# Two-layer diffusion trunk: per-token sums of squares of the differential attention by ScalarE, values turned back on TensorE, swapped rope rows by DMA, maps turned three blocks behind their scores

## What is computed

```python
q, k, v = split(h @ w_in, 3)
q = q * d ** -0.5                      # d = 64
q, k = rope(q), rope(k)                # latent tokens only; rotates pairs 16 rows apart
s = einsum('bqhjd,bshjd->bhjqs', q, k) # two maps a head, j = 0, 1
p = softmax(s)
a = p[:, :, 0] - lam_full * p[:, :, 1]
o = einsum('bhqs,bshe->bqhe', a, v)
o = rms(o) * subln_g * (1 - lam_init)  # over the 128 values of a head
out = o.reshape(B, T, D) @ w_out
```

## Time and profile before

| | |
|---|---|
| median of 3 runs | 1935.22 us (1934.19 to 1935.46) |
| the profiled execution's own time | 1935.05 us |
| its span, first to last instruction | 1933.4 us |
| mean granted TensorE clock | 0.991 |
| busy, share of the span | TensorE 98%, VectorE 59%, ScalarE 34%, GpSimd 7% |
| diff_v, by the trace | 492.6 to 547.1 us |
| diff_attn, by the trace | 547.9 to 640.6 us |
| down's row-by-row chunk | 640.6 to 654.3 us |

### The profile page before, as it was taken

The page is one execution under the profiler, slowest core; times in us unless marked ns, Lnnn a source line. Parts: engine busy times, 40 slices in busy tenths (PEclk is TensorE's granted clock), DMA queues, the critical chain, the costliest instruction groups (busy, mean ns, idle before and its releaser), DMA issues.

```text
span 1933.4 us, 29212 instructions
## 1 busy us (share of the span) xinstructions
PE 1893.6 (98%) x10896; PEld 1659.1 (86%) x10896; DVE 1143.6 (59%) x1858; ACT 665.9 (34%) x1052; POOL 136.5 (7%) x196
## 2 busy tenths in 40 slices
PE   8999999999989999999999999999999999999998
PEld 6888888898955898888889888888898998989998
DVE  7887772263468478777424777752362534655554
ACT  5322322242257343223223322232243322544442
POOL 0001000000001211000000110100100000010000
PEclk9999999999989999999999999999999999999999
DMA  8466543244210136666332566633343220545554
GB/s 314 157 209 193 184 151 104 90 129 138 88 44 1 45 111 214 195 196 183 103 106 88 178 207 194 195 106 105 92 153 126 93 87 22 175 153 174 185 164 129
DMA packets 80861, 269.75 MB, mean 140 GB/s; under 512 B 8977, under 2 KB 14353, under 8 KB 80785
## 3 DMA queue, kind: packets, MB, share of 16 engines
q1 hardware_dynamic: 62354, 201.58, 32.0%
q0 software_dynamic: 18432, 67.12, 11.4%
HBM read 267.62 MB, written 1.05 MB: 139 GB/s over the span
## 4 chain that ended last, share of the span: by engine, by line
PE 92%; DVE 5%; issue 1%; DMA 1%; ACT 0%; SPq 0%; POOL 0%; POOLq 0%; DVEq 0%; ACTq 0%
PE pt L1267 23%; PE pt L1270 23%; PE pt L1268 23%; PE pt L1393 3%; PE pt L1502 2%; PE pt L1503 2%; PE pt L1504 2%; PE pt L1629 2%; PE pt L1631 2%; PE pt L1630 2%; PE pt L1569 1%; PE pt L1397 1%; PE pt L1333 1%; PE pt L1535 1%; DVE wl L774 1%
## 5 line engine op out<-in xcount | busy, mean ns | idle before, releaser
L774 DVE TENSOR_TENSOR wl<-raw,wh 128x1024 fp32r<-128x1024 f32 (+2 forms) x394 | 432.4, 1137 | 511.7 <-ACT wh L542 507.8
L1267 PE MATMUL pt<-xh,wh 128*128 128x512 f32 (+1 forms) x1632 | 584.9, 358 | 0.2 <-DVE wl L774 0.2
L1268 PE MATMUL pt<-xh,wl 128*128 128x512 f32 (+1 forms) x1632 | 584.1, 358 | 0.0
L1270 PE MATMUL pt<-xl,wh 128*128 128x512 f32 (+1 forms) x1632 | 582.7, 358 | 0.0
L542 ACT CAST wh<-raw 128x1024 fp32r<-128x1024 f32 (+2 forms) x394 | 364.1, 970 | 243.9 <-PE pt L1270 188.8
L1270 PEld LDWEIGHTS pt<-xl,wh 128*128 128x128 f32 x1632 | 308.3, 189 | 45.0
L1268 PEld LDWEIGHTS pt<-xh,wl 128*128 128x128 f32 x1632 | 308.4, 189 | 44.9
L1267 PEld LDWEIGHTS pt<-xh,wh 128*128 128x128 f32 x1632 | 308.4, 189 | 44.9 <-issue 0.3
L786 DVE CUSTOM_DVE_ANT_0 pt<-modw,raw 128x1024 f32<-128x1024 f32 x256 | 305.7, 1255 | 10.8 <-DMA modw<-in_mod_rows 10.8
L1267 PE MATMUL pt<-uh,wh 128*128 128x512 f32 (+1 forms) x572 | 203.9, 356 | 0.0
L1268 PE MATMUL pt<-uh,wl 128*128 128x512 f32 (+1 forms) x572 | 203.9, 356 | 0.0
(11 more groups left out here) (186 smaller groups left out, 2308.4 us busy)
## 6 DMA issues: line engine op xcount, KB each, us to landing
raw<-in_ffn_w SPq DMA_DIRECT2D x238, 512.0 KB, 4.0
modw<-in_mod_rows POOLq DMA_DIRECT2D x128, 512.0 KB, 4.6
raw<-in_ret_w_in SPq DMA_DIRECT2D x48, 512.0 KB, 4.4
raw<-in_diff_w_in SPq DMA_DIRECT2D x24, 512.0 KB, 4.3
raw<-in_ffn_w SPq DMA_DIRECT2D x32, 256.0 KB, 3.9
raw<-in_ret_w_out SPq DMA_DIRECT2D x16, 512.0 KB, 4.1
region<-in_mod_rows SPq DMA_DIRECT2D x8, 512.0 KB, 14.6
region<-in_mod_start SPq DMA_DIRECT2D x8, 512.0 KB, 15.2
```

Of the source, the lines that this page charges most:

```text
L774: nc.vector.tensor_tensor(flat(wl[:, s, cut]), raw[:, raw_slot(late, s, p), 0:part_rows * CW], flat(wh[:, s, cut].bitcast(F32)), ALU.subtr ...
L1267: nc.tensor.matmul(bank, w_hi[:, k, cut], hi(k), start=a, stop=False)
L1268: nc.tensor.matmul(bank, w_lo[:, k, cut], hi(k), start=False, stop=False)
L1270: return nc.tensor.matmul(bank, w_hi[:, k, cut], lo(k), start=False, stop=b)
```

## The change

1. The swapped rows no longer come from TensorE. GpSimd issues 32 DMAs after the last copy-out of diff_qk, each 16 partitions x 4 tiles x 256 tokens (64 KB), from `qk` to a new tile `other_rows`, eight for each group of four tiles; `rope` waits for its group and reads `other_rows`. The permutation matmuls go, and so does TensorE's wait for `roped` between them.
2. 1/8 moves from the exponentials' scale into q's copy-out; the row maxima are taken with the sign turned, straight into the bias, and the multiplication behind them goes.
3. `values` takes the turned maps as weights and `vd` as the moving side: the output has tokens on the partitions, 128 x 128 a matmul, twice as many matmuls of half the width.
4. The squares are summed along the free side by ScalarE, four 128 x 128 activations a head with an accumulated sum; `orawd` and its copy go, and `sum_head` and `spread_head` too. VectorE scales by four per-partition factors, a broadcast operand, straight from PSUM, TensorE turns the scaled tile back (`turn_head`, four transposes), ScalarE and VectorE take the high and the low part from PSUM with `subg` as scale.
5. Turning and everything behind it come one block later: at step v TensorE turns block v - 3, ScalarE copies it, and values, squares, means, scaling, turning back, high and low parts follow from there (squares at 8, mean at 9, scale at 10, the rest at 13). In down the turnings of heads 6 and 7 stand in front of rows 1 and 4.
6. A second, equal wait on GpSimd's queue near the kernel's start goes.

```diff
-AT_SUM, AT_SPREAD = 9, 11
-AT_SQUARE, AT_HI, AT_LO = 7, 12, 13
+TURN_LAG = 3
+AT_SQUARE, AT_HI = TURN_LAG + 5, TURN_LAG + 10
+AT_MEAN, AT_SCALE, AT_LO = TURN_LAG + 6, TURN_LAG + 7, TURN_LAG + 10
+AT_TURN = TURN_LAG + 10
 V_STEPS = 4 * (DH - 1) + AT_HI + 1
...
+        for s in range(2):
+            pool.wait_ge(evac[s], 2 * (ph["sa"], ph["sb"])[s])
+        n = DD // 4
+        for g in range(4):
+            for b in range(P // n):
+                pool.dma_start(other_rows[b * n:(b + 1) * n, 4 * g:4 * g + 4, :],
+                               qk[(b ^ 1) * n:((b ^ 1) + 1) * n, 4 * g:4 * g + 4, 0:LAT]).then_inc(swap_landed[g], 16)
     if kind == "down":
         clear(ph)
...
-def copy_out(ph, dst, T, i, s):
+def copy_out(ph, dst, T, i, s, factor=1.0):
     for t in range(2):
         tile_done((ph["sa"], ph["sb"])[s] + i, s, t, 2 * (ph["q"] + i) + s)
-        nc.scalar.copy(row(dst, 4 * i + 2 * s + t)[:, 0:T], pt[:, 2 * s + t, 0:T]).then_inc(evac[s], 1)
+        nc.scalar.activation(row(dst, 4 * i + 2 * s + t)[:, 0:T], pt[:, 2 * s + t, 0:T], ACT.Copy,
+                             scale=factor).then_inc(evac[s], 1)
...
                 copy_out(ph, dst, T, 1, s)
             continue
-        with act.Fori(0, (2 if kind != "diff_qk" else 4)) as i:
+        if kind == "diff_qk":
+            with act.Fori(0, 2) as i:
+                for s in range(2):
+                    copy_out(ph, dst, T, i, s, factor=DD ** -0.5)
+        with act.Fori(2 if kind == "diff_qk" else 0, 4 if kind == "diff_qk" else 2) as i:
             for s in range(2):
                 copy_out(ph, dst, T, i, s)
...
+                nc.scalar.activation(ex(u, b)[:, j, 0:nk], pt[:, 2 * b + j, 0:nk], ACT.Exp,
                                      bias=shift[:, 2 * b + j:2 * b + j + 1],
                                      accum_out=masses(u, b)[:, j:j + 1]).then_inc(exped, 1)
         def turn_out(u, b):
...
             act.wait_ge(pv_done, 2 * h + 2)
             if h >= 2:
-                act.wait_ge(o_summed, h - 1)
-            nc.scalar.activation(tmp[:, h % 2, :], pt[:, 5 + h % 2, :], ACT.Square).then_inc(o_squared, 1)
-            nc.scalar.copy(orawd[:, h, :], pt[:, 5 + h % 2, :]).then_inc(o_copied, 1)
+                act.wait_ge(hvar_ready, h - 1)
+            for b in range(TT):
+                at = TT * (h % 2) + b
+                nc.scalar.activation(tmp[:, 0, b * P:(b + 1) * P], pt[:, 5 + h % 2, b * P:(b + 1) * P], ACT.Square,
+                                     accum_out=o_sums[:, at:at + 1]).then_inc(o_squared, 1)
         def hi_o(h):
-            act.wait_ge(o_scaled, h + 1)
-            nc.scalar.copy(xh[:, h, :], tmp[:, 2 + h % 2, :]).then_inc(o_hi, 1)
+            act.wait_ge(o_turned, h + 1)
+            nc.scalar.activation(xh[:, h, :], pt[:, SUM, :], ACT.Copy, scale=subg).then_inc(o_hi, 1)
         for v in range(V_STEPS):
-            if 2 <= v < V + 2:
-                turn_out((v - 2) // 2, v % 2)
+            if TURN_LAG <= v < V + TURN_LAG:
+                turn_out((v - TURN_LAG) // 2, (v - TURN_LAG) % 2)
...
             decay_products(0)
             decay_products(1)
         def rope(r, bank, tile):
-            dve.wait_ge(swapped, r + 1)
-            nc.vector.tensor_tensor(tmp[:, bank % 2, 0:LAT], pt[:, bank, 0:LAT], droped[:, 1], ALU.mult).then_inc(rope_terms, 1)
+            dve.wait_ge(swap_landed[r // 4], 16 * P * 4 // DD)
+            nc.vector.tensor_tensor(tmp[:, bank % 2, 0:LAT], other_rows[:, r, :], droped[:, 1], ALU.mult).then_inc(rope_terms, 1)
             nc.vector.tensor_tensor(tile, tile, droped[:, 0], ALU.mult).then_inc(rope_terms, 1)
             dve.wait_ge(rope_terms, 2 * r + 2)
...
             nk = TOK if u % 2 == 0 else CTX
             dve.wait_ge(scored, 2 * u + b + 1)
-            nc.vector.tensor_reduce(top[:, 2 * b:2 * b + 2], pt[:, 2 * b:2 * b + 2, 0:nk], AX.X, ALU.max).then_inc(topped, 1)
-            dve.wait_ge(topped, 2 * u + b + 1)
-            nc.vector.tensor_scalar(shift[:, 2 * b:2 * b + 2], top[:, 2 * b:2 * b + 2], -(DD ** -0.5), None,
-                                    ALU.mult).then_inc(shifted, 1)
+            nc.vector.tensor_reduce(shift[:, 2 * b:2 * b + 2], pt[:, 2 * b:2 * b + 2, 0:nk], AX.X, ALU.max,
+                                    negate=True).then_inc(shifted, 1)
         def mix(u, b):
...
         def mean_o(h):
-            dve.wait_ge(o_summed, h + 1)
+            dve.wait_ge(o_squared, TT * (h + 1))
             dve.wait_ge(mass_squared, h + 1)
-            nc.vector.scalar_tensor_tensor(hvar[:, TT * h:TT * (h + 1)], pt[:, SUM, 0:TT], 1.0 / P,
+            nc.vector.scalar_tensor_tensor(hvar[:, TT * h:TT * (h + 1)], o_sums[:, TT * (h % 2):TT * (h % 2 + 1)], 1.0 / P,
                                            mass_eps[:, TT * (h % 2):TT * (h % 2 + 1)], ALU.mult,
                                            ALU.add).then_inc(hvar_ready, 1)
         def scale_o(h):
-            dve.wait_ge(hbcast_ready, h + 1)
-            dve.wait_ge(o_copied, h + 1)
+            dve.wait_ge(hrstd_ready, h + 1)
             if h >= 2:
-                dve.wait_ge(x_ready, ph["x"] + h - 1)
-            nc.vector.scalar_tensor_tensor(tmp[:, 2 + h % 2, :], orawd[:, h, :], subg, pt[:, SUM, :],
-                                           ALU.mult, ALU.mult).then_inc(o_scaled, 1)
+                dve.wait_ge(o_turned, h - 1)
+            factors = hrstd[:, TT * h:TT * (h + 1)].rearrange("p (b o) -> p b o", o=1).broadcast_to([P, TT, P])
+            nc.vector.tensor_tensor(tmp[:, 2 + h % 2, :].rearrange("p (b d) -> p b d", b=TT),
+                                    pt[:, 5 + h % 2, :].rearrange("p (b d) -> p b d", b=TT), factors,
+                                    ALU.mult).then_inc(o_scaled, 1)
         def lo_o(h):
             dve.wait_ge(o_hi, h + 1)
-            nc.vector.tensor_tensor(xl[:, h, :], tmp[:, 2 + h % 2, :], xh[:, h, :].bitcast(F32),
-                                    ALU.subtract).then_inc(x_ready, 1)
+            nc.vector.scalar_tensor_tensor(xl[:, h, :], pt[:, SUM, :], subg, xh[:, h, :].bitcast(F32),
+                                           ALU.mult, ALU.subtract).then_inc(x_ready, 1)
         for v in range(V_STEPS):
             if v < V:
                 mix(v // 2, v % 2)
                 if v % 4 == 3:
...
     ins.then_inc(scored, 1)
-def sum_head(h):
-    pe.wait_ge(o_squared, h + 1)
+head_x = next(ph["x"] for ph in phases if ph["kind"] == "diff_attn")
+def turn_head(h):
+    pe.wait_ge(o_scaled, h + 1)
     if h:
-        pe.wait_ge(o_scaled, h)
+        pe.wait_ge(x_ready, head_x + h)
     for b in range(TT):
-        ins = nc.tensor.matmul(pt[:, SUM, b:b + 1], tmp[:, h % 2, b * P:(b + 1) * P],
-                               ones[:, 0:1], start=True, stop=True)
-    ins.then_inc(o_summed, 1)
-def spread_head(h):
-    pe.wait_ge(hrstd_ready, h + 1)
-    for b in range(TT):
-        column = hrstd[:, TT * h + b:TT * h + b + 1]
-        ins = nc.tensor.matmul(pt[:, SUM, b * P:(b + 1) * P], column.broadcast_to([P, P]), ident,
-                               start=True, stop=True)
-    ins.then_inc(hbcast_ready, 1)
+        cut = slice(b * P, (b + 1) * P)
+        ins = nc.tensor.transpose(pt[:, SUM, cut], tmp[:, 2 + h % 2, cut], ident)
+    ins.then_inc(o_turned, 1)
...
-                for e in range(4 if diff else 0):
-                    r = 8 * i + 4 * s + e
-                    if not (first and s == 0):
-                        pe.wait_ge(roped, r - 3)
-                    nc.tensor.matmul(pt[:, 4 + e, 0:LAT], swap_d, row(qk, r)[:, 0:LAT], start=True,
-                                     stop=True).then_inc(swapped, 1)
                 for n in range(TT):
...
             if g == 0 and h >= 2:
-                pe.wait_ge(o_copied, h - 1)
-            for k in range(k0, TT):
-                ins = nc.tensor.matmul(pt[:, 5 + h % 2, g * LAT:(g + 1) * LAT], vd[:, k, h * P:(h + 1) * P],
-                                       aTd[:, u % 2, k, :], start=(k == k0), stop=(k == TT - 1))
+                pe.wait_ge(o_scaled, h - 1)
+            for b in range(LAT // P):
+                at = g * LAT + b * P
+                for k in range(k0, TT):
+                    ins = nc.tensor.matmul(pt[:, 5 + h % 2, at:at + P], aTd[:, u % 2, k, b * P:(b + 1) * P],
+                                           vd[:, k, h * P:(h + 1) * P], start=(k == k0), stop=(k == TT - 1))
             ins.then_inc(pv_done, 1)
...
                 score(v // 2, v % 2)
-            if 2 <= v < V + 2:
-                turn_probs(v // 2 - 1, v % 2)
-            if 4 <= v < V + 4 and v % 2 == 0:
-                values(v // 2 - 2)
-            for at, step in ((AT_SUM, sum_head), (AT_SPREAD, spread_head)):
-                if at <= v < at + 4 * DH and (v - at) % 4 == 0 and v < at + 4 * DH - (8 if step is spread_head else 4):
-                    step((v - at) // 4)
+            if TURN_LAG <= v < V + TURN_LAG:
+                turn_probs((v - TURN_LAG) // 2, (v - TURN_LAG) % 2)
```

(34 more changed lines are left out.)

## The result

The changed kernel takes 1913.87 us, the median of four runs (1912.61 to 1915.68), against 1935.34 us for the kernel before in the same series (four runs, 1934.19 to 1935.69). The ratio is 0.9891, 95% interval 0.9874 to 0.9908: 1.1% faster, 21.5 us.

The account below looks back on a forecast made before the run. TensorE, with 92% of the chain, was taken as the bound, alternating with VectorE in the attention. Gains of 6.9 + 7.7 + 1.6 = 16.2 us gave 1919.0 us, range 1914 to 1926.

Parts of the forecast that it names:

- Permutations: In diff_v, sixteen permutations leave TensorE's chain, four per chunk at 1.73 us: 6.9 us gained, the replacing DMAs costed at nothing.
- the limit near 1.2 us: In diff_v, the DMAs are free up to 1.19 us an issue on GpSimd's queue; 0.64 was expected.
- the estimate of 1950: Kernel time if the 64 KB DMAs, 2.15 us each by the Trainium skill, did not overlap: 1919.0 + 31 us.
- Attention: TensorE drops out of the head's loop, which closes through ScalarE and VectorE: 9.9 us a head against 11.01, 7.7 us gained.
- I take 0.40: One 128-wide square on ScalarE in the attention loop: 0.40 us, bounds 0.30 and 0.47, four a head making 1.6.
- The opening and the end: In the attention, the opening's gain and the end's loss, each 1 to 2 us, set against each other at nothing.
- The floor: Attention bounded by VectorE alone: 78.9 us busy less 32 x 0.17, over eight heads, 9.2 us a head, gaining 12.6.
- Down's chunk: Down's first chunk: two spreadings and a sum go, 2.57 us, two turnings of 0.5 come: 1.6 us gained.
- Scale and sign: Factor in q's copy-out costs nothing; sign inside the row-maximum reduction costs between nothing and 0.17 us, taken as nothing.
- B: In diff_v, DMAs come late and VectorE's rotation holds up products; all gain gone at 1.70 us an issue; chance 10%.
- C: ScalarE's squares close the attention loop at 0.6 us each: 10.7 us a head, time 1924.6; chance 14%.
- D: In the attention stage, less TensorE work doubles the time at 1.2 GHz (granted clock 0.92 before): 1928 us; chance 8%.

Follow-up runs that it names:

- experiment 3: Kernel before with only the 32 DMAs in place of the sixteen permutation matmuls: 1928.87 us, ratio 0.9973.
- experiment 4: Changed kernel with each of the 32 DMAs cut into four of 16 KB, 128 in all: 1934.84 us.
- experiment 1: Changed kernel with the maps turned two blocks behind their scores instead of three: 1922.61 us, ratio to before 0.9940.
- experiment 2: Kernel before with the lag of three blocks alone, all steps of the heads one block later: 1924.06 us, ratio 0.9944.
- experiment 5: Changed kernel with four more 128x128 squares and sums a head on ScalarE, results unread: 1926.86 us.
- experiment 6: Changed kernel with the row maximum in two steps again, reduction then multiplication by -1: 1916.41 us.
- experiment 8: Changed kernel with the high part one block and the low part two blocks behind their turning back: 1911.16 us.
- experiments 7 to 10: Changed kernel with half the squares a block later and turning back earlier, high and low parts later, or both (two versions): 1910.95, 1911.16, 1912.49, 1913.23 us.

## Why the prediction was right, and where it was off

- **Permutations**, forecast 6.9 us at no cost beside: 6.9 in the trace, 5.5 on the whole by experiment 3. The first group of rows was used at 503.40 us, forecast 503.4, by luck: the issues took 0.51 us instead of 0.64, and the landings of this group up to 6.1 us instead of 4.6. VectorE had waited 6.7 us for it with nothing behind it that was needed. The step that decided, issues well under the limit near 1.2 us, held, and experiment 4 bears the limit out by the estimate of 1.27. The Trainium skill's fixed 2.0 us a transfer ("DMA: Bandwidth & Descriptors", anatomy of a DMA on the GpSimd path) agrees with the shortest landing of the 64 KB transfers here, 2.2 us, not with those of 16 KB in experiment 4, 1.6 us at the shortest and 1.9 in the median, where the measurement decides. 32 transfers of 64 KB were issued in 16.25 us, so the fixed parts overlapped, and the estimate of 1950 that hung on their standing one behind another did not come about.
- **Attention**, forecast 7.7 us, measured 14.2. The mechanism was the forecast one: TensorE left the loop (experiments 1 and 2), and the new loop goes through exponentials, squares and VectorE (the chain above, experiment 5). The forecast named TensorE's lighter work beside the lag without a price for either; by experiment 2 the lag alone gives 11.2, and by experiment 6 the lighter work shows a gain behind it only together with the one-step maximum. Mis-sized was the term "I take 0.40" for a square. The timeline shows them 0.25 us apart:

```profile
588.56 0.28 ACT L744 ACTIVATE tmp<-pt 128x128 f32<-128x128 f32 x1
588.72 0.21 ACT L744 ACTIVATION_READ_ACCUMULATOR tmp<-pt 128x1 f32 x1
588.81 0.28 ACT L744 ACTIVATE tmp<-pt 128x128 f32<-128x128 f32 x1
588.97 0.22 ACT L744 ACTIVATION_READ_ACCUMULATOR tmp<-pt 128x1 f32 x1
```

  That is below the lower bound of 0.30: the line through the two exponentials, 0.37 at 128 columns, doesn't hold for these squares; why is not shown. 4 x 0.15 = 0.6 us a head makes 9.9 into 9.3 (measured 9.28) and 7.7 into 11.9, and seven periods of 11.01 - 9.28 would give 12.1. The sum behind the 9.9 has a slip of 0.1: VectorE's terms with four hand-overs add up to 5.4, not "5.3 or less". The rest of the 14.2 is about 2 us: the two stretches at the lower clock inside the loop, which the forecast had taken to stay, cost about that (1.1 shown, the other estimated). The opening and the end were set against each other at nothing, a gain and a loss of 1 to 2 us each. Measured, the opening with the first period gives 1.8 us, about a period's worth, and the end 1.1, about what the second low stretch costs: each came out near nothing.
- **The floor**, "VectorE alone, 9.2 us", was not one: experiment 8 runs at 8.79. The 78.9 us busy of the earlier trace rows hold 4.0 us that are not the heads', two low parts of weights (2.4, L774) and the last rotation (1.6, L1105 to L1108). Without them it is (78.9 - 4.0 - 5.4) / 8 = 8.7 us a head, and the range would have begun 3.5 us lower. Of the range's two ends it was this that left the result out by 0.1 us.
- **Down's chunk**, forecast 1.6 us, measured 2.0. Head 7's turning was not waited for. In the stream a turning takes 0.35 us to the next product instead of the 0.5 set for it.
- **Scale and sign**: the removed multiplication got no term of its own; it is only absent from the loop's sum, so its 3.2 us (experiment 6) were in the forecast 9.9 without being told apart.
- **Rivals**: B was open only past 1.2 us an issue; C, squares of 0.6, went the other way; D, more time at 1.2 GHz, also: 0.97 over the stage instead of 0.92. That the low stretches inside the loop went with the waits for the mix would be a wrong reading: experiment 1 has 13.3 us of these waits and no such stretch, experiment 5 has one and no such waits, and they come and go between executions of one kernel. What brings them stays open.

## What to carry to other kernels

Where two engines of one loop both stand idle in it (here 1.3 and 1.6 us of each 11.0), look for the instruction that waits for work its partner has only just finished, and move it back one step in its queue: one block of lag was worth 11.2 us of the attention's 14.2 by itself, and all the removed work behind it 3.0. The next link can have other loops close behind it: two repairs gave 2.0 and 2.7 us, and both together 1.8. Small DMAs were free here as long as the time to issue them fitted beside other work; the number of issues decided, not the bytes. Before dividing a stage's busy time into a floor for one head, take out of it what the heads do not do.

## What the runs showed of the hardware

GpSimd's power of four columns got faster without being touched: 1.38 us before, 1.01 us after.

```profile
597.08 1.38 POOL L525 TENSOR_TENSOR small<-small 128x4 f32<-128x4 f32 x1 [9.62 <-DVE small L1173]
```

```profile
592.71 1.01 POOL L537 TENSOR_TENSOR small<-small 128x4 f32<-128x4 f32 x1 [8.28 <-DVE small L1192]
```

Each time VectorE's low part runs beside it. Before, that was a `tensor_tensor` with both inputs in SBUF; after, an operation with one input in PSUM. The kernel before has the short form too: its first power has no low part beside it.

```profile
575.58 1.03 POOL L525 TENSOR_TENSOR small<-small 128x4 f32<-128x4 f32 x1 [127.06 <-DVE small L1173]
```

Its other seven powers, each with the low part beside it, take 1.38 or 1.39 us. In the changed kernel a power takes the same 1.01 us with its low part beside it and, in experiments 7 to 10, without. The Trainium skill ("GPSIMD Engine Reference", Specifications) says that GpSimd shares its SBUF interface with VectorE and contends with instructions of two SBUF inputs. The traces agree; no run here changed this alone.
